# A two-block transformer kernel: another order of the first loads, three steps placed elsewhere, one norm's sums on VectorE

## The reference, cut to what matters

```python
# first block, layer 0 (gated linear recurrence) and layer 1 (differential attention)
h = h + rms_norm(hgrn2_mixer(rms_norm(h, a_norm_pre), a_w_in, ...), a_norm_post)
h = h + rms_norm(squared_relu_mlp(rms_norm(h, mlp_norm_pre0), up0, down0), mlp_norm_post0)
k, v = shared_kv(h, kv_norm, w_kv)                 # rms_norm(h, kv_norm) @ w_kv
h = h + rms_norm(diff_attn_mixer(rms_norm(h, b_norm_pre), k, v, b_w_q, ...), b_norm_post)
h = h + rms_norm(squared_relu_mlp(rms_norm(h, mlp_norm_pre1), up1, down1), mlp_norm_post1)
# second block: window attention and a state-space branch on one input projection
p = rmsnorm(h, norm_mix) @ w_in
merged = sigmoid(gate_a) * (windowed_gqa_sink(q, k, v, sink) @ w_attn_branch) \
       + sigmoid(gate_b) * (ssd_branch(z, xbc, dt, ...) @ w_ssd_branch)
h = h + merged @ w_out
h = h + cross_attention(rmsnorm(h, norm_cross), rmsnorm(mem, norm_mem), ...)
h = h + square(relu(rmsnorm(h, norm_ffn) @ w_up)) @ w_down
out = rmsnorm(h, norm_final)
```

## Time and profile before

| | us |
|---|---|
| median of 3 runs | 2617.7 |
| the profiled execution, its own time | 2614.55 |
| its span in the profile | 2612.7 |
| TensorE busy in the span | 2532.8 |
| VectorE, ScalarE, GpSimd busy | 1474.9, 1160.1, 155.1 |
| mean granted TensorE clock | 0.992 |

### The profile page before, as it was taken

How to read it: one execution, slowest core, us unless ns; L and a number is a source line. 1 busy time by engine, 2 the same in 40 slices (tenths; PEclk the granted TensorE clock), 3 DMA queues, 4 the chain that set the end, 5 groups by cost and what they waited for, 6 DMA issues and landing times.

```text
span 2612.7 us, 31879 instructions
## 1 busy us (share of the span) xinstructions
PE 2532.8 (97%) x12440; PEld 2063.3 (79%) x12440; DVE 1474.9 (56%) x2377; ACT 1160.1 (44%) x2087; POOL 155.1 (6%) x149
## 2 busy tenths in 40 slices
PE   7999999999999999999989999999999999999998
PEld 5888778888776678888867888888877787788886
DVE  5555464334566655344368888886666566543343
ACT  4254443223356645233247666665455444442232
POOL 1110010000010000000010010000000010000000
PEclk9999999999999999999999999999999999999999
DMA  4212124435232222322323212222312243233222
GB/s 133 73 57 65 57 75 125 117 107 127 81 104 72 77 68 89 105 97 89 99 63 105 64 58 65 73 71 84 92 58 62 70 142 99 73 105 97 97 97 73
DMA packets 196790, 226.24 MB, mean 87 GB/s; under 512 B 7393, under 2 KB 132609, under 8 KB 196385
## 3 DMA queue, kind: packets, MB, share of 16 engines
q1 hardware_dynamic: 196640, 224.21, 28.2%
HBM read 214.22 MB, written 9.44 MB: 86 GB/s over the span
## 4 chain that ended last, share of the span: by engine, by line
PE 81%; DVE 11%; ACT 5%; issue 2%; DMA 0%; POOL 0%; DVEq 0%; SPq 0%; ACTq 0%; POOLq 0%
PE bank L1886 22%; PE bank L1887 22%; PE bank L1888 22%; DVE CV L2597 2%; PE bank L1892 2%; DVE wlo L2371 2%; PE bank L1893 2%; PE bank L1894 2%; PE bank L1928 1%; ACT whi L2153 1%; PE bank L1905 1%; PE bank L2085 1%; PE bank L2093 1%; PE bank L2061 1%; PE bank L1992 1%
## 5 line engine op out<-in xcount | busy, mean ns | idle before, releaser
L2371 DVE TENSOR_TENSOR wlo<-raw,whi 128x1024 fp32r<-128x1024 f32 x389 | 484.1, 1250 | 664.8 <-ACT whi L2153 662.2
L2153 ACT ACTIVATE whi<-raw 128x1024 fp32r<-128x1024 f32 x389 | 409.1, 1058 | 592.7 <-PE bank L1888 576.7
L1886 PE MATMUL bank<-XAh,whi 128*128 128x512 f32 x1536 | 614.9, 400 | 16.7 <-DVE XAl L2379 4.8
L1888 PE MATMUL bank<-XAh,wlo 128*128 128x512 f32 x1536 | 601.6, 392 | 0.0
L1887 PE MATMUL bank<-XAl,whi 128*128 128x512 f32 x1536 | 601.4, 392 | 0.0
L1886 PEld LDWEIGHTS bank<-XAh,whi 128*128 128x128 f32 x1536 | 290.2, 189 | 94.7 <-issue 28.6
L1888 PEld LDWEIGHTS bank<-XAh,wlo 128*128 128x128 f32 x1536 | 290.1, 189 | 62.3
L1887 PEld LDWEIGHTS bank<-XAl,whi 128*128 128x128 f32 x1536 | 290.6, 189 | 58.7 <-issue 0.7
L1886 PE MATMUL bank<-XBh,whi 128*128 128x512 f32 x824 | 327.8, 398 | 2.9 <-DVE XBl L2377 1.7
L1887 PE MATMUL bank<-XBl,whi 128*128 128x512 f32 x824 | 321.7, 390 | 0.0
L1888 PE MATMUL bank<-XBh,wlo 128*128 128x512 f32 x824 | 321.6, 390 | 0.0
(11 more groups left out here) (338 smaller groups left out, 3374.2 us busy)
## 6 DMA issues: line engine op xcount, KB each, us to landing
raw<-in_w_in SPq DMA_DIRECT2D x77, 512.0 KB, 3.8
raw<-in_up SPq DMA_DIRECT2D x64, 512.0 KB, 3.5
raw<-in_down SPq DMA_DIRECT2D x64, 512.0 KB, 3.6
raw<-in_a_w_in SPq DMA_DIRECT2D x32, 512.0 KB, 3.9
raw<-in_w_up SPq DMA_DIRECT2D x32, 512.0 KB, 3.7
raw<-in_w_down SPq DMA_DIRECT2D x32, 512.0 KB, 3.7
raw<-in_w_kv SPq DMA_DIRECT2D x16, 512.0 KB, 3.5
raw<-in_w_ssd_branch SPq DMA_DIRECT2D x16, 512.0 KB, 3.3
```

Source lines behind the costliest of these rows:

```text
L1886: pe.matmul(out, wh[:, w, c], xh[:, x, 0:s.ntok], start=st, stop=False)
L1888: m = pe.matmul(out, wl[:, w, c], xh[:, x, 0:s.ntok], start=False, stop=en)
L2153: act.activation(s.hi, s.raw, ACT.Copy).then_inc(s.whi[0], 1)
L2371: dve.tensor_tensor(s.lo, s.raw, s.hi.bitcast(F32), ALU.subtract).then_inc(s.wlo[0], 1)
```

## The change

It does six things. (1) The gain columns of the constants are loaded by themselves and first, then weight unit 0, two tiles of h, unit 1, two tiles, unit 2, two tiles, the rest of the constants in two transfers, the last two tiles; the split of unit 0 is put ahead of the first tile's. (2) VectorE sets a temporary tile to ones, and TensorE makes four products of it at once; `setup` moves to the sixth tile; for the first two units the weight splits are placed one unit later in the order. (3) Layer 0's XA is made by `norm_tiles`, and the two value units stand ahead of its first tile and behind its second. (4) The fourth piece of the first key product goes ahead of `rcol`. (5) The sum of squares for norm_mix is added by VectorE. (6) `wi_exp` is cut in two: the maximum stays in its slot (`wi_top`), the exponentials go one slot later.

```diff
-    def norm_tiles(X, src, ready, g, fac, nk=8, n=S, every=0):
+    def norm_tiles(X, src, ready, g, fac, nk=8, n=S, every=0, room=1):
...
-                while not tmps.room(1):
+                while not tmps.room(room):
...
-    add("setup", cst_in=p.sig("cst_in", 16), lam=sig("lam"), lb=sig("lb"), eps=sig("eps"),
...
-    load_x = Step(kind="load_x", land=list(ht))
+    K.gain_in, K.cst_in = sig("gain_in", 16), sig("cst_in", 32)
+    load_gain, load_cst = Step(kind="load_gain", land=K.gain_in), Step(kind="load_cst", land=K.cst_in)
+    load_x = [Step(kind="load_x", k=k, land=ht[k]) for k in range(8)]
+    b, t = ring_all.take(), tmps.take()
+    s = add("first_warm", bank=b, t=t, n=4, filled=sig("filled"), warm=sig("first.warm"))
...
         for k in range(8):
-            split(XB, k, hsrc(k), ht[k], scale=col(gain["a_norm_pre"] + k), src2=K.cst_in)
+            if k == 5:
+                s = add("setup", lam=sig("lam"), lb=sig("lb"), eps=sig("eps"), lam1=sig("lam1"), lam2=sig("lam2"), lb1=sig("lb1"), lb2=sig("lb2"))
...
+            split(XB, k, hsrc(k), ht[k], scale=col(gain["a_norm_pre"] + k), src2=K.gain_in)
...
         def products():
             r, rt = fac0["r"], fac0["t"]
-            for k in range(8):
-                while not tmps.room(3):
-                    yield WAIT
-                t = tmps.take()
-                v = add("scaled", src=hsrc(k), src_ready=ht[k], gain=col(gain["a_norm_pre"] + k), r=r, rfin=rt, t=t, n=S, scaled=sig("scaled")).scaled
-                t.free(split(XA, k, t.t[:, :], v))
-                if k in (1, 5):
-                    next(g0)
-                yield
-            r.free(v, s1.mm, *fac0["used"])
+            rows = norm_tiles(XA, hsrc, ht, gain["a_norm_pre"], (r, rt), room=3)
+            next(g0)
+            yield
+            done = 0
+            for got in rows:
+                yield got
+                if got != WAIT:
+                    done += 1
+                    if done == 2:
+                        next(g0)
+            r.free(*r.slot.after, s1.mm, *fac0["used"])
...
         f = rms_close(b, ones(b), D)
+        assert next(gk) != WAIT
         b = ring_all.take()
...
-    nxt, squares, ones = into(XB, "norm_mix_2", early=True)
+    nxt, squares, ones = into(XB, "norm_mix_2", by="sq_add_v", early=True)
...
-            begun, exps, normed = p.pieces, [], []
-            for x in range(2):
-                exps.append(add("wi_exp", s=ss[x], ...
-                yield
-                yield from p.spaced(1)
-            for x in range(2):
-                normed.append(add("wi_norm", s=ss[x], ...
+            f, normed = [], []
+            for x in range(4):
+                if x < 2:
+                    f.append(dict(s=ss[x], c=stw[:, 2 * hp + x, :], hd=2 * hp + x, slope=slopes[x], biased=s2.biased[x], top=sig("wi.top"), exp=sig("wi.exp")))
+                    add("wi_top", **f[x])
+                if 0 < x < 3:
+                    add("wi_exp", **f[x - 1])
+                if x > 1:
+                    normed.append(add("wi_norm", s=ss[x - 2], c=stw[:, 2 * hp + x - 2, :], exp=f[x - 2]["exp"], normed=sig("wi.norm")).normed)
                 yield
                 yield from p.spaced(1)
...
-    order = [p.order[0]] + loads[0] + [load_x] + [x for n in range(1, NRAW) for x in loads[n]]
-    placed = 0
+    order = [load_gain, p.order[0]] + loads[0] + load_x[0:2] + loads[1] + load_x[2:4] + loads[2] + load_x[4:6] + [load_cst] + load_x[6:8] + [splits[0]] + loads[NRAW]
+    placed = 1
...
-            while placed < min(s.n + NW, len(splits)):
+            while placed < min(s.n + (NW if s.n > 1 else 2), len(splits)):
...
+        elif k == "first_warm":
+            on.wait_ge(*s.filled)
+            on.room(s.bank)
+            for _ in range(s.n):
+                m = pe.matmul(s.bank.t[:, :], s.t.t[:, 0:P], s.t.t[:, :], start=True, stop=True)
+            m.then_inc(s.warm[0], 1)
...
-            sp.dma_start(K.cst[:, :], io["cst"]).then_inc(s.cst_in[0], 16)
+        elif k == "load_gain":
+            sp.dma_start(K.cst[:, C_GAIN:C_CONVW], io["cst"][:, C_GAIN:C_CONVW]).then_inc(s.land[0], 16)
```

More of the change, by code:

```diff
@@ L2410, in dve_program @@
             dve.tensor_copy(s.dst, s.src).then_inc(s.copied[0], 1)
+        elif k == "first_warm":
+            on.room(s.t)
+            dve.memset(s.t.t[:, :], 1.0).then_inc(s.filled[0], 1)
         elif k == "setup":
             dve.memset(K.epst[:, :], EPS).then_inc(s.eps[0], 1)
-            on.wait_ge(*s.cst_in)
+            on.wait_ge(*K.cst_in)
             lw, ls2, lamc = K.lwork, K.ls2, K.lamc
@@ L2775, in sp_program @@
             sp.dma_start(s.dst, s.src).then_inc(s.land[0], 16)
-        elif k == "setup":
-            sp.dma_start(K.cst[:, :], io["cst"]).then_inc(s.cst_in[0], 16)
+        elif k == "load_gain":
+            sp.dma_start(K.cst[:, C_GAIN:C_CONVW], io["cst"][:, C_GAIN:C_CONVW]).then_inc(s.land[0], 16)
+        elif k == "load_cst":
+            sp.dma_start(K.cst[:, 0:C_GAIN], io["cst"][:, 0:C_GAIN]).then_inc(s.land[0], 16)
+            sp.dma_start(K.cst[:, C_CONVW:NCST], io["cst"][:, C_CONVW:NCST]).then_inc(s.land[0], 16)
         elif k == "load_x":
-            for n in range(8):
-                sp.dma_start(K.h[:, n, :], io["xT"][:, n, :]).then_inc(s.land[n][0], 16)
+            sp.dma_start(K.h[:, s.k, :], io["xT"][:, s.k, :]).then_inc(s.land[0], 16)
         elif k == "load_tab":
@@ L2821, in sp_program @@
             sp.wait_ge(sem, plan.sent[name])
-DMA_SIGNALS = {"cst_in", "tab_in", "bias_in", "rows", "T0", "T1", "spill", "rel_in", "mem_in", "out"} | {f"{x}{k}" for x in "hx" for k in range(8)}
+DMA_SIGNALS = {"gain_in", "cst_in", "tab_in", "bias_in", "rows", "T0", "T1", "spill", "rel_in", "mem_in", "out"} | {f"{x}{k}" for x in "hx" for k in range(8)}
 def program(nc, io, out_d):
```

9 lines of the change are left out of this document (4 added, 5 removed).

## The result

The changed kernel takes **2594.8 us** in the median of 4 runs (2590.1 to 2596.7), the kernel before 2617.75 beside it: a ratio of 0.991, with a 95% interval of 0.9893 to 0.9927, or 23.0 us less. The forecast was 2596.3. The profiled execution of the changed kernel took 2596.09 us (span 2594.3) against 2614.55: 18.4 us between the two executions that can be compared row by row.

What follows compares the result with a forecast made beforehand. TensorE was taken as the bound, busy 2532.8 of 2612.7 us, with gains only in its standing and lower-clock time. Terms 7.9 + 4.4 + 1.4 + 2.9 + 4.8 = 21.4 us off the 2617.7 median gave 2596.3, range 2588 to 2606.

Steps and rivals of the forecast that it cites:

- Opening: Start of the kernel: new load order and products of ones bring `ones` from 32.28 to 24.4; 7.9 us, bounds 3.6 to 9.
- byte model: Opening: landing times from bytes queued ahead, at 0.25 then 0.38 MB/us; first weight unit 4.9, first tile 5.7.
- term for the clock: Opening: products of ones raise TensorE's clock before the real matmuls, so 13 slow matmuls run at full pace; 2.7 us.
- XA: Layer 0's XA: a tile every 1.35 us, the 1.37 us query gate wait gone; 4.4 us, bounds 0 to 6.5.
- Key piece: First key product: twelve matmuls fill TensorE's wait for the norm's factor at `rcol`; 1.4 us, bounds 0 to 1.5.
- Sums: norm_mix: adds moved from GpSimd to VectorE cut a tile from 3.31 to 2.8 us; 2.9 us, bounds -1 to 4.
- Exponentials: Window attention: exponentials a slot later remove most of 5.3 us of TensorE waits; 4.8 us, bounds 1.5 to 5.5.
- rival of a slower window attention: Each second head's division makes TensorE wait 2.75 us in eight pairs, 22.0 lost, 4.8 not won: 2623.1; chance 0.02.
- half opening: Rival: h lands no sooner after issue, clock low at the first real matmuls; opening gives 3.6: 2600.6; chance 0.15.
- lost XA: Rival: XA gives nothing, value evacuations hold ScalarE and the clock falls; half the exponentials' gain stays: 2603.1; chance 0.13.
- mere shifting: Rival: behind each stage VectorE's head chains set the pace, only the opening counts, about 8 us: 2609.7; chance 0.05.
- better case: Rival: all bounds at their good ends, 26.5 us won: 2591.2; chance 0.03.

Runs made afterwards that it cites:

- changed_again: The changed kernel, unaltered, run once more for a second trace: 2593.96 us, ratio 0.9913.
- old_loads: The changed kernel with the old load order (all constants, weight unit 0, all of h, units 1 and 2): 2598.21 us, ratio 0.9922.
- old_xa: The changed kernel with layer 0's XA made by the loop of the kernel before, value units after tiles 2 and 6: 2600.56 us, ratio 0.9927.
- xa_old_units: The changed kernel, keeping the pipelined XA tiles, with the value units back behind tiles 2 and 6: 2594.55 us, ratio 0.9911.
- key_behind: The changed kernel with the fourth piece of the key product back behind `rcol`: 2594.52 us, ratio 0.9921.
- sums_gpsimd: The changed kernel with the sum of squares for norm_mix given back to GpSimd: 2593.65 us, ratio 0.9918.
- exp_alone: The kernel before with only the exponentials of window attention moved one slot later: 2611.41 us (10 runs) beside 2616.84, ratio 0.9978.
- warm4: The changed kernel with four products of ones, instead of two, in each pause ahead of an MLP's stage: 2591.49 us, ratio 0.9904.
- mem_halves: The kernel with four products of ones per MLP pause, plus cross attention's memory load cut into two halves with own semaphores: 2591.77 us, ratio 0.9906.
- no_first_ones: The changed kernel with the four opening products of ones cut to one product of two columns: 2594.71 us, ratio 0.9907.

## Why the forecast was right, step by step

The total (21.4 us forecast, 23.0 measured in the medians, 18.4 between the two traces) came out for the reasons given; each of the five terms, if not every piece of it, is shown by an experiment that takes its part back. That the median came within 1.5 us of the forecast is in part luck: the forecast for the profiled execution was 2593.2, and it took 2596.09; low stretches move a single execution by a few us either way; and the errors of the terms have both signs. The sizes of the terms:

- **Opening, 7.9 forecast, 7.6 measured** at `ones`, 6.7 in changed_again, where the first weight unit was used at 6.02 instead of 5.12. The byte model held to 0.8 us (first tile 5.7 forecast, used at 6.42), in changed_again to 1.1 (weight unit 4.9 forecast, used at 6.02), and the matmul start to 0.3 and 1.2. The term for the clock was 2.7 and its worth is 2.2. Its working was off and did no harm: by the forecast's own figures the products of ones end at 8.1 (1.8 us of work at the lower level left at 7.2 is 0.9 at the higher), not at 7.8 and not ahead of the first real matmul at 7.9. They ended at 6.73, for the clock rose sooner than after 5.7 us: four products take 3.76 us at the higher level, so about 3.0 of the 5.28 us were at the lower one (an estimate). What the forecast didn't foresee is that old_loads would show the order of the transfers as nearly the whole of it (6.4 us): without it the clock falls again. What the later `setup` and the other order of the splits give was not tried by itself.
- **XA, 4.4 forecast, 4.7 measured** (12.24 at the SC wait less 7.58 at `ones`), about 1.3 of it a low stretch that the kernel before had there (the seven matmuls from 63.98 on take 3.01 us instead of about 1.7). The tile takes 1.26 us (1.35 forecast); the third is done at 47.09 and the eighth at 53.00, which is 54.7 and 60.6 on the forecast's axis (54.3 and 60.3). Taken from `ones`, old_xa gives 5.3 with a low stretch and 3.7 without. The share given to the gate's wait is not shown: xa_old_units has a longer one and loses only by the clock.
- **Key piece, 1.4 forecast, 1.2 measured**, and up to 4.6 in an execution whose clock falls behind the wait (key_behind). The upper bound of 1.5 was too low for such an execution: it priced the wait and not what may follow it.
- **Sums, 2.9 forecast, 2.3 measured** (sums_gpsimd against the changed kernel, without low clock); between the first two traces *sums* gave 3.9, of which about 1.5 is a low stretch at 1354 in the kernel before. The tile is 2.82 us, the forecast 2.8; the step that was a little too large is the last, from five tiles to when TensorE starts.
- **Exponentials, 4.8 forecast, 5.4 to 5.9 measured** by exp_alone (median, and *attention* with one low stretch each). Between the two traces it was 3.2: the changed kernel had a wait of 1.3 us at 2104, which part 6 does not cause (exp_alone), and one low stretch more. The forecast's "new waits" were looked for between 64 and 313; this one stood at the end of the stage. The rival of a slower window attention found nothing for it: no wait for SW in any trace with the new order.

The five measured terms make 7.6 + 4.7 + 1.2 + 2.3 + 5.9 = 21.7 us. From trace to trace, the four distances give 12.2 + 1.2 + 3.9 + 3.2 = 20.5, and 1.5 and 0.9 us of low clock at 1510 and 2142 in the changed kernel, that the kernel before had not, take back 2.4; that leaves 18.1 of the 18.4, and the rest of the program is 0.3 us shorter. What remains open is the 1.3 us by which the medians show more than the sum: it is inside their spread.

Of the rivals, the half opening is refuted by the start at 8.24 and the full clock, the lost XA by waits of 0.3 us, the mere shifting by *opening* to *key*, 396.6 us in every trace: TensorE keeps each gain of the opening to that point. The slower window attention is refuted too: no trace of the new slots has a wait for SW. The better case (2591.2) did not come, since no term but the last passed its forecast by more than 0.3 us.

## What to carry to other kernels

Where one engine is busy for 97% of the span, price a change by the distance between two waits that both traces share, stage by stage; here a median of four runs could not tell a part of 2 us from nothing, and the distances agreed within 0.15 us where no low stretch fell into them. Ask of each wait of the bounding engine whether the time behind it is paced by that engine: a wait removed where it paces is won whole (window attention), while the clock regained behind a pause is worth nothing where the next wait, for another engine, takes it up (warm4). A queue should not hold a step that waits for a transfer in front of one that the bounding engine needs soon; with half the transfer to wait for, a wait that had been 0.1 to 2.6 us in other traces was not there (mem_halves, one trace).

## What had not been expected of the hardware

- **The stretches of lower clock belong to the execution.** Two traces of one kernel have ten and six; all fourteen traces between three and twelve, the one at the very end left out. They begin behind waits of TensorE, but not behind each. Where TensorE paces, one costs about 1.5 us (at 1510: 53.05 against 51.55 us for the same stretch of work). The runs of a kernel spread by 1 to 8 us, and the clock goes along: of 13 runs of the kernel before, the fastest (2613.3 us) has a mean granted clock of 0.993, the slowest (2620.9) of 0.990.
- **The granted clock reads 1.00 before its first change**, even where matmuls of 512 columns start 0.43 us apart (no_first_ones, 8.5 to 12.5 us). The pace tells the level.
- **The four products of ones at the start took 5.28 to 6.76 us** in eleven traces. At the higher level they would take 3.76, so the lower one lasted between about 3.0 and 6.0 us (an estimate: each us above 3.76 is two at half speed). In ten of the traces TensorE then stood for 0 to 2.1 us and the real matmuls ran at the higher clock from the first on; behind the 3.9 us of old_loads it fell again some six matmuls later.
- **A VectorE addition that starts behind one of GpSimd waits for its end**, also when the two share no data: in both experiments it ends 0.55 us behind it, although it otherwise takes 0.68 in all.
